# Keys scaled by POOL, a slab's low part made in pieces, a slab asked for sooner, and products of ones at the start

## The chip, the cores and the metric

The kernel runs on one core of a Trainium2 chip. The metric is the device time of one execution in microseconds. PE is TensorE, DVE VectorE, ACT ScalarE, POOL GpSimd; SP issues the transfers.

## The reference

The input is 512 rows of 1024 features in float32. The first block norms them, makes two attentions (one of a window of 128, one of a two-dimensional neighbourhood), gates and merges them, and adds a feed-forward part of width 4096. The second block runs two layers of this form:

```python
for l in range(2):
    p = rms_norm(x, norm_g[l]) @ w_in[l]
    c_q, c_kv, k_pe, z_a, u_f, z_f, g_a, g_f = split(p)
    q = rms_norm(c_q) @ w_uq                     # 8 heads x 96
    k_nope, v = split(rms_norm(c_kv) @ w_ukv)    # 8 heads x (64 + 64)
    k = concat(k_nope, k_pe for every head)      # 8 heads x 96
    q, k = rope(rms_norm(q, q_head_g)), rope(rms_norm(k, k_head_g))
    o_a = softmax(q k^T * 96**-0.5) @ v
    y_a = (o_a * silu(z_a)) @ w_attn_proj
    y_f = (real(fft2(u_f)) * silu(z_f)) @ w_fourier_proj
    m = sigmoid(g_a + b[0]) * y_a + sigmoid(g_f + b[1]) * y_f
    x = x + m @ w_out
```

## The kernel before, in words

**Split products.** Every float32 operand is split into a high part (ACT copies it to fp32r) and a low part (the difference), and each product is three passes of PE, `PASSES`. Activations lie with features on the partitions. Weights come as slabs of 128x2048 numbers, 1 MB each, numbered by `j`. Slab `j` lands in `K.raw[:, j % 2]`; ACT writes its high part to `K.w[:, j % 2, 0]` (`split`, L872) and counts `w_hi`; DVE writes the low part to `K.w[:, j % 2, 1]` (`split`, L1164) and counts `w_lo`. PE waits for `w_lo` in `slab_ready` and makes two tiles of 128x512 from most slabs (L1694), 24 products of 512 columns a tile. SP asks for slab `j` when the low part of slab `j - 2` is done, since it overwrites that buffer.

**Order.** There is no scheduler: each engine runs one list of instructions in the order of its program, and waits on counting semaphores. What stands behind a waiting instruction on its engine waits too.

**The start.** SP loads the input and the first weights in four pairs, in pieces of 0.5 MB. PE turns the input with the identity (`x_turned`, L1848), ACT and DVE split it and the weights piece by piece, and PE multiplies (`qa_part`, L1857). `K.ones` is set by POOL (L699) and first used for the sums of squares (`stat_sum`, `stat_spread`). SP's list then has slabs 2 and 3, some 25 small loads (gains, masks, rope, head gains), the bias table of the second attention through device memory in three transfers that wait for each other (zero it, write `rpb`, spread the rows), slab 4, the bias rows of two heads, and slabs 5 to 8. Tiles 4 and 5 come from slab 2, tiles 6 and 7 from slab 3, 8 and 9 from slab 4, and so on.

**A layer of block 2, to its attention.** PE makes the latents, queries (8 tiles), keys with values (8 tiles), then eight tiles from slabs `j + 5` to `j + 8`: 0 to 3 are the Fourier input, 4 to 7 the gate `z`. Meanwhile ACT squares the heads (`hsq`), DVE sums the squares (L1582), makes the roots (`head_roots`, L1565) and writes the tiles (`normed`, L1203); POOL multiplies gains in and rotates (`gain`, `rotate`), then makes `silu` of the four `z` tiles (`silu_f`, L801). The query's root is multiplied into the scores, but the keys themselves are scaled: `key_scale` on DVE (L1573), two instructions of 128x1536 numbers, after `z` tiles 5 and 6. The semaphore `head_scaled` counts the roots and both scalings. Four banks of PSUM take PE's tiles in turn, so a group can start only when DVE has emptied the one four before it.

**The Fourier stage** follows the list `FOURIER`: `dim` multiplies a group by the 128-point matrix (two banks each), `seq` by the 512-point one (slab `j + 9`, `dft_seq`), and `turn` transposes head 0's queries and keys. ACT and DVE split what `dim` gives into `ab` (L1123, L1622). At the first `seq` ACT and DVE split slab `j + 10`, which PE needs only after the attention.

**The attention** (`Heads`, kind L) has 32 steps `n`, four a head. For each, PE makes scores of 128x512, DVE scales them and finds the extreme of each row (L1302), ACT exponentiates, DVE inverts the sum (`rden`), POOL multiplies it in (`probabilities`, L718), PE transposes (`transposes`, L1778), ACT and DVE split the result (L964, L1328), and PE multiplies by the values (L1797). Heads are turned two ahead: in the step after `n % 4 == 2`, PE turns head `n // 4 + 2`. In layer 0 POOL also multiplies a tile of `x` after every even step (`scaled_x`, L742 up to step 14, L747 after it).

These are the functions that the change touches.

Of the kernel before, what the change touches and what calls it, by code (L numbers as in the profile page):

```python
# [13 lines left out]
F32 = mybir.dt.float32  # L14
# [52 lines left out]
QA_PIECES = 2 * HALF  # L67
QA_MORE = QA_PIECES - 2
J_L, JL = 57, 28
J_END = J_L + LAYERS * JL  # L70
# [22 lines left out]

KEY_SCALE = {5: 0, 6: 1}
PAR_DMAS = 6 + LAYERS * 9
# [70 lines left out]
def allocate(nc, ctx, K):  # L166
# [3 lines left out]
    def semaphore(name):  # L170
        return ctx.enter_context(nc.semaphore(name))
# [168 lines left out]
    K.head_rec = semaphore("head_rec")  # L340
    K.head_scaled = semaphore("head_scaled")
    K.rope_ok = semaphore("rope_ok")
    K.qk_ready = semaphore("qk_ready")
# [90 lines left out]
class Heads:  # L434


    def __init__(self, K, kind, layer=0):
        self.kind, self.layer = kind, layer
        self.u0 = {"AB": Num(U_A), "L": Num(U_L, (layer, UL))}[kind]
        self.s0 = {"AB": Num(S_A), "L": Num(S_L + 4, (layer, SL))}[kind]  # L440
        self.g0 = {"AB": Num(G_A), "L": Num(G_L + 40, (layer, GL))}[kind]
        self.total = len(kind) * HEADS * TT
        self.scaled = Num(3, (layer, 3))
        self.qk0 = Num(0, (layer, 2 * HEADS))
        self.f0 = Num(F_L + 40, (layer, FL)) if kind == "L" else None
        self.K = K
# [72 lines left out]
def program_sync(nc, sp, K):  # L519
# [61 lines left out]

    in_slab(2)
    in_slab(3)
    for i, gain in ((1, a["norm_mlp"][0]), (2, a["norm_final"])):
# [10 lines left out]
    for l in range(LAYERS):  # L595
# [7 lines left out]
        for q, g in enumerate((a["q_head_g_2"], a["k_head_g_2"])):  # L603
            sp.dma_start(K.head_gain[0:NOPE, q, l:l + 1], g[l][0:NOPE].rearrange("(k p) -> p k", p=NOPE),
                         allow_slow_non_contiguous=True).then_inc(K.par_in, 16)

    sp.wait_ge(K.zero_ok, 1)
    sp.dma_start(K.tab.rearrange("(p n) -> p n", p=P), K.zero[:, :]).then_inc(K.tab_zeroed, 16)
# [13 lines left out]

    in_slab(4)
    sp.wait_ge(K.rows_in, 16)
    for h in range(2):
        bias_rows(h)
    for j in range(5, 9):
        in_slab(j)
# [68 lines left out]
def program_pool(nc, pool, K):  # L697
# [13 lines left out]
    def probabilities(A):  # L711

        for n in range(A.total):
            _, _, _, lo, hi = A.where(n)
            c = slice(A.first(n), A.first(n) + (hi - lo) * P)
            pool.wait_ge(K.rden_ok, (A.u0 + n + 1).value())
            p = K.t[:, n % 3, c]
            nc.gpsimd.tensor_tensor(p, p, K.rden[:, n % 4:n % 4 + 1].broadcast_to([P, (hi - lo) * P]),  # L718
                                    ALU.mult).then_inc(K.probs_ok, 1)
            if A.kind == "L" and A.layer == 0 and n % 2 == 0:  # L720
                scaled_x(n // 2)
            if A.at(n) == "B":
                b = n - HEADS * TT
                if b == 1:
                    clear_b(0)
                if b == 3:
                    clear_b(1)
                if b // TT + 1 >= 2 and b // TT + 1 < HEADS and b % TT < 3:
                    masked(b // TT + 1, b % TT)
# [47 lines left out]
    def rotate(l, q, i):  # L777
# [18 lines left out]
        nc.gpsimd.tensor_tensor(x2, x2, ra, ALU.add).then_inc(K.rope_ok, 1)  # L796

    def silu_f(l, t):

        pool.wait_ge(K.sig_ok, (sig_num(l, t) + 1).value())  # L800
        nc.gpsimd.tensor_tensor(K.z[:, t, :], K.z[:, t, :], sig_f(K, t), ALU.mult).then_inc(K.pool_ok, 1)  # L801
# [24 lines left out]
    for l in range(LAYERS):  # L826
# [8 lines left out]
        for t in range(4):  # L835
            silu_f(l, t)
        probabilities(Heads(K, "L", l))

# [22 lines left out]
def program_act(nc, act, K):  # L861
# [201 lines left out]
    for l in range(LAYERS):  # L1063
# [26 lines left out]
        for i in range(4):  # L1090
            if i != 2:
                split(j + 6 + i, f + 20 + 2 * i)
            for k in range(2 * i, 2 * i + 2):
                for n in HEAD_SQUARES[k]:
                    q, t = divmod(n, TT)
# [63 lines left out]
def program_vector(nc, dve, K):  # L1159
# [316 lines left out]
    for l in range(LAYERS):  # L1476
# [90 lines left out]

        def key_scale(i):

            dve.wait_ge(K.rope_ok, Num(12 + 6 * (i + 1), (l, 24)).value())  # L1570
            v = K.qk[:, 1, 2 * i:2 * i + 2, :].rearrange("p t (h c) -> p (t h) c", h=HEADS)
            r = K.hr[:, 1, 2 * i * HEADS:(2 * i + 2) * HEADS]
            nc.vector.tensor_tensor(v, v, r.unsqueeze(2).broadcast_to([P, 2 * HEADS, QK]),  # L1573
                                    ALU.mult).then_inc(K.head_scaled, 1)

        for i in range(4):
            if i != 2:
                split(j + 6 + i)
            for k in range(2 * i, 2 * i + 2):
# [25 lines left out]
                if k == HEAD_ROOT:  # L1605
                    head_roots()
                if k in KEY_SCALE:
                    key_scale(KEY_SCALE[k])
        def branch_lo(grp):
# [3 lines left out]
        for stage, grp in FOURIER:  # L1613
            if (stage, grp) == ("seq", 0):
                split(j + 10)
            if stage == "dim":
# [23 lines left out]
        def za_lo(t):  # L1640
            lo(K.v[:, 1, t, :], K.t[:, t % 3, :], K.v[:, 0, t, :], h + 20 + t)

        for i in range(2):
            split(j + 11 + i)
# [27 lines left out]
def program_pe(nc, pe, K):  # L1672
# [63 lines left out]
    def turn(A, h):  # L1736

        for q in range(2):
            b = bank(A.g_qk(h) + q)
# [111 lines left out]
    def qa_part(k, t):  # L1851
# [7 lines left out]
        return mm  # L1859

    pe.wait_ge(K.ident_in, 16)
    pe.wait_ge(K.gain_in, 16)
# [3 lines left out]
    for k in range(HALF):  # L1866
# [4 lines left out]
        for i in ((2, 3), (4,), (5, 6), (7,))[k]:  # L1871
            x_turned(i)
    pe.wait_ge(K.ones_ok, 1)
    for t in range(HALF):
# [48 lines left out]
    for l in range(LAYERS):  # L1923
# [48 lines left out]
        for stage, grp in FOURIER:  # L1972
# [8 lines left out]
            elif stage == "turn":  # L1981
                pe.wait_ge(K.head_scaled, Num(3, (l, 3)).value())
                turn(heads, grp)
# [96 lines left out]
```

## Time and profile before

| | |
|---|---|
| median of three runs | 1535.9 us (1533.59 to 1538.47) |
| the profiled execution, its own time | 1537.36 us |
| its span, first to last instruction | 1535.6 us |
| mean granted clock of PE | 0.992 |
| PE busy | 1503.5 us, 98% |
| DVE busy | 818.8 us, 53% |
| ACT busy | 609.5 us, 40% |
| POOL busy | 339.1 us, 22% |
| DMA moved | 125.97 MB |

Busy is the union of an engine's instruction times. The ends of PE's instructions are modelled, so a row's length is a little more than the time to the next row's start. The granted clock is a share of full speed. "Idle before" is the time that an engine stood still ahead of an instruction, with what released it.

### The profile page before, as it was taken

To read this page: it belongs to the slowest core of one execution; us is meant where nothing else is said; L and a number is where in the kernel's file an instruction comes from. 1 tells how busy PE (TensorE), PEld (TensorE's weight loads), DVE (VectorE), ACT (ScalarE), POOL (GpSimd) and SP (SyncE) were. 2 spreads that over 40 slices of the span, in tenths; PEclk is the share of its full clock that TensorE was granted. 3 is DMA by queue.
4 is the path that set the end of the run, shared out by engine and by line. 5 is a ranking of instruction groups with operands and counts; after the bars stand their busy time and mean duration, and the time that the engine had idled before them with its cause. 6 is when DMAs were issued, how large, how long until landed. Compare 5 with 4: busy or idle time off the path is not lost.

```text
span 1535.6 us, 18967 instructions
## 1 busy us (share of the span) xinstructions
PE 1503.5 (98%) x7247; PEld 1248.4 (81%) x7247; DVE 818.8 (53%) x1324; ACT 609.5 (40%) x931; POOL 339.1 (22%) x338
## 2 busy tenths in 40 slices
PE   8899999999999999999999899999999999999998
PEld 6787788888888888888888788888888879888886
DVE  5437764344543433334578695444447879643444
ACT  5225772324331313234434575332333447533232
POOL 2004560001100000001308275110120724421012
PEclk9999999999999999999999999999999999999999
DMA  5511003332233232323232002323223200232321
GB/s 170 130 57 58 22 22 101 108 104 99 83 110 110 83 110 82 109 82 103 69 110 82 1 1 83 110 83 106 87 84 115 83 0 1 83 110 83 101 92 56
DMA packets 136478, 125.97 MB, mean 82 GB/s; under 512 B 20807, under 2 KB 132687, under 8 KB 136399
## 3 DMA queue, kind: packets, MB, share of 16 engines
q1 hardware_dynamic: 136239, 124.83, 26.1%
q8 instruction: 52, 0.85, 0.2%
q14 instruction: 27, 0.22, 0.0%
q10 hardware_dynamic: 160, 0.07, 0.0%
HBM read 122.75 MB, written 2.39 MB: 81 GB/s over the span
## 4 chain that ended last, share of the span: by engine, by line
PE 87%; DVE 6%; ACT 1%; issue 1%; SPq 1%; DMA 1%; POOL 1%; ACTq 0%; DVEq 0%; POOLq 0%
PE G L1694 67%; PE S L1676 5%; PE G L1676 5%; PE G L1797 5%; PE T L1778 3%; DVE w L1164 1%; ACT w L872 1%; PE G L1741 1%; POOL t L718 1%; PE G L1857 1%; DVE hs L1582 0%; DVE sq L1556 0%; DVE u L1177 0%; DVE sq L1302 0%; DMA raw<-in_w_in 0%
## 5 line engine op out<-in xcount | busy, mean ns | idle before, releaser
L1694 PE MATMUL G<-gx,w 128*128 128x512 f32 x3024 | 696.5, 391 | 5.2 <-DVE w L1164 5.2
L1694 PEld LDWEIGHTS G<-gx,w 128*128 128x128 f32 x3024 | 568.7, 188 | 125.4 <-DVE w L1164 5.7
L1164 DVE TENSOR_TENSOR w<-raw,w 128x2048 fp32r<-128x2048 f32 x112 | 257.6, 2300 | 236.5 <-ACT w L872 236.5
L872 ACT ACTIVATE w<-raw 128x2048 fp32r<-128x2048 f32 x112 | 211.6, 1889 | 147.8 <-PE G L1694 109.4
L1694 PE MATMUL G<-kvb,w 128*128 128x512 f32 x960 | 218.4, 389 | 0.0
L1694 PEld LDWEIGHTS G<-kvb,w 128*128 128x128 f32 x960 | 180.2, 188 | 37.4
L718 POOL TENSOR_TENSOR t<-t,rden 128x512 f32<-128x512 f32 (+2 forms) x128 | 109.5, 857 | 129.0 <-DVE rden L1308 128.7
L764 POOL TENSOR_TENSOR t<-sig 128x512 f32<-128x512 f32 x24 | 35.3, 1472 | 357.4 <-DVE sig L1377 357.4
L1429 DVE TENSOR_TENSOR x<-G,x 128x512 f32<-128x512 f32 x56 | 38.6, 689 | 114.9 <-PE G L1694 114.9
L934 ACT ACTIVATE t<-sq,nm 128x512 f32<-128x512 f32 (+3 forms) x128 | 80.2, 627 | 28.6 <-DVE nm L1302 27.7
L1694 PE MATMUL G<-m,w 128*128 128x512 f32 x384 | 87.4, 389 | 0.0
L1694 PEld LDWEIGHTS G<-m,w 128*128 128x128 f32 x384 | 72.1, 188 | 15.0
L1203 DVE SCALAR_TENSOR_TENSOR sig<-G,rstd 128x512 f32<-128x512 f32 x48 | 33.0, 687 | 95.1 <-PE G L1694 95.1
L825 POOL TENSOR_TENSOR sumsq_f<-sumsq_f,sq_f 128x512 f32<-128x512 f32 x7 | 9.1, 1299 | 333.4 <-ACT sq_f L902 333.4
L1778 PE MATMUL T<-ident,t 128*128 128x128 f32 x400 | 68.8, 284 | 4.1 <-POOL t L718 4.0
L1778 PEld LDWEIGHTS T<-ident,t 128*128 128x128 f32 x400 | 45.5, 140 | 26.0 <-POOL t L718 9.2
L972 ACT ACTIVATE sig<-sig,lp 128x512 f32<-128x512 f32 x32 | 23.2, 725 | 108.2 <-DVE sig L1203 108.2
L709 POOL TENSOR_TENSOR sumsq<-sumsq,sq 128x512 f32<-128x512 f32 x28 | 37.7, 1345 | 122.3 <-ACT sq L890 104.2
L1049 ACT ACTIVATE sq<-t 128x512 f32<-128x512 f32 x32 | 20.2, 632 | 110.8 <-DVE t L1452 110.8
L1676 PE MATMUL S<-ab 96*128 96x512 f32 x192 | 57.4, 409 | 0.7 <-DVE nm L1302 0.7
L1328 DVE TENSOR_TENSOR pt<-T,pt 128x256 fp32r<-128x256 f32 (+2 forms) x96 | 50.6, 527 | 7.1 <-ACT pt L964 3.4
L1377 DVE TENSOR_TENSOR sig<-G,sig 128x512 f32<-128x512 f32 x48 | 32.0, 687 | 40.9 <-PE G L1694 40.9
(219 smaller groups left out, 1777.4 us busy)
## 6 DMA issues: line engine op xcount, KB each, us to landing
raw<-in_w_in SPq DMA_DIRECT2D x98, 512.0 KB, 7.1
raw<-in_w_up SPq DMA_DIRECT2D x32, 512.0 KB
raw<-in_w_down SPq DMA_DIRECT2D x32, 512.0 KB
raw<-in_w_out SPq DMA_DIRECT2D x24, 512.0 KB
raw<-in_w_attn_proj SPq DMA_DIRECT2D x8, 512.0 KB
raw<-in_w_fourier_proj SPq DMA_DIRECT2D x8, 512.0 KB
xin<-in_x SPq DMA_DIRECT2D x4, 512.0 KB, 6.4
raw<-in_w_proj_a SPq DMA_DIRECT2D x8, 256.0 KB
```

What stands on the lines that cost most here:

```text
L709: nc.gpsimd.tensor_tensor(K.sumsq[:, :], K.sumsq[:, :], K.sq[:, k % 2, :], ALU.add).then_inc(K.sum_ok, 1)
L718: nc.gpsimd.tensor_tensor(p, p, K.rden[:, n % 4:n % 4 + 1].broadcast_to([P, (hi - lo) * P]), ALU.mult).then_inc(K.probs_ok, 1)
L764: nc.gpsimd.tensor_tensor(K.t[:, m, :], sig[:, m, :], sig[:, 2 + m, :], ALU.add).then_inc(K.mix_ok, 1)
L872: nc.scalar.activation(K.w[:, j % 2, 0, 0:n], K.raw[:, j % 2, 0:n], ACT.Copy).then_inc(K.w_hi, 1)
L934: nc.scalar.activation(K.t[:, n % 3, 0:width], K.sq[:, n % 2, 0:width], ACT.Exp, bias=K.nm[:, n % 4:n % 4 + 1], scale=-1.0, accum_out=K.de ...
L1164: nc.vector.tensor_tensor(K.w[:, s, 1, 0:n], K.raw[:, s, 0:n], K.w[:, s, 0, 0:n].bitcast(F32), ALU.subtract).then_inc(K.w_lo, 1)
L1328: nc.vector.tensor_tensor(K.pt[A.at(n)][m % 2][:, 1, b0:b1, e, :], K.T[(U + n) % 2][:, 0:(b1 - b0) * P].rearrange("p (k c) -> p k c", c=P) ...
L1429: nc.vector.tensor_tensor(K.x[:, k, :], psum(g)[:, :], K.x[:, k, :], ALU.add).then_inc(K.tile_out, 1)
L1676: mm = nc.tensor.matmul(bank, lhs, rhs, start=(i == 0), stop=(i == len(pairs) - 1))
L1694: mm = nc.tensor.matmul(b[:, :], w(p, k), x(q, k), start=(k == i == 0), stop=(k == kts - 1 and i == len(PASSES) - 1))
L1778: mm = nc.tensor.transpose(K.T[(U + n) % 2][:, k * P:(k + 1) * P], K.t[:, n % 3, c:c + P], K.ident[:, :])
L1797: mm = nc.tensor.matmul(out[:, :, :], v, K.pt[kind][m % 2][:, q, k, :, :], start=(i == p == q == 0), stop=(k == b1 - 1 and (p, q) == PASSE ...
```

## The change

It has four parts.

1. PE waits for the ones and multiplies them 11 times by themselves into a bank that is not read, ahead of its first transpose.
2. SP asks for slab 4 directly behind slab 3, and for slab 5 behind the small loads, ahead of the bias table; slabs 6 to 8 stay behind the first bias rows.
3. The keys of block 2 are scaled by POOL, head by head (all four row tiles of one head, 4x96 numbers a partition): heads 0 and 1 between the `silu` tiles, heads 2 to 7 within the attention. PE waits for a head's count `key_ok` when it turns it. ACT splits the slab `j + 9` ahead of its work for `z` tile 5 instead of ahead of tile 6.
4. The low part of slab `j + 10` is made by POOL in four pieces of 128x512 behind the probabilities of steps 3, 5, 7 and 9. DVE waits for it after the attention.

```diff
@@ SP
-    in_slab(2)
-    in_slab(3)
+    for j in range(2, 5):
+        in_slab(j)
...
+    in_slab(5)
     sp.wait_ge(K.zero_ok, 1)
     sp.dma_start(K.tab.rearrange("(p n) -> p n", p=P), K.zero[:, :]).then_inc(K.tab_zeroed, 16)
...
-    in_slab(4)
     sp.wait_ge(K.rows_in, 16)
     for h in range(2):
         bias_rows(h)
-    for j in range(5, 9):
+    for j in range(6, 9):
         in_slab(j)
@@ POOL, probabilities
+            if A.kind == "L" and n % TT == 1 and n // TT + 2 < HEADS:
+                key_scaled(A.layer, n // TT + 2)
+            if A.kind == "L" and n in LOW_AT:
+                slab_low(A.layer, LOW_AT.index(n))
@@ POOL
+    def key_scaled(l, h):
+
+        if h == 0:
+            pool.wait_ge(K.head_scaled, l + 1)
+            pool.wait_ge(K.rope_ok, 24 * (l + 1))
+        v = K.qk[:, 1, :, h * QK:(h + 1) * QK]
+        r = K.hr[:, 1, :].rearrange("p (t h) -> p t h", t=TT)[:, :, h:h + 1]
+        nc.gpsimd.tensor_tensor(v, v, r.broadcast_to([P, TT, QK]), ALU.mult).then_inc(K.key_ok, 1)
+
+    def slab_low(l, i):
+
+        j = Num(J_L + 10, (l, JL))
+        s, n = j % 2, SLAB // len(LOW_AT)
+        c = slice(i * n, (i + 1) * n)
+        if i == 0:
+            pool.wait_ge(K.w_hi, (j + 1 + QA_MORE).value())
+        if i == len(LOW_AT) - 1:
+            pool.wait_ge(K.w_lo, (j + QA_MORE).value())
+            pool.wait_ge(K.low_ok, (len(LOW_AT) - 1) * (l + 1))
+        nc.gpsimd.tensor_tensor(K.w[:, s, 1, c], K.raw[:, s, c], K.w[:, s, 0, c].bitcast(F32),
+                                ALU.subtract).then_inc(K.w_lo if i == len(LOW_AT) - 1 else K.low_ok, 1)
...
         for t in range(4):
             silu_f(l, t)
+            if t % 2:
+                key_scaled(l, t // 2)
@@ ACT, layers
         for i in range(4):
-            if i != 2:
+            if i < 2:
                 split(j + 6 + i, f + 20 + 2 * i)
             for k in range(2 * i, 2 * i + 2):
+                if k == 5:
+                    split(j + 9, f + 26)
@@ DVE, layers
-        def key_scale(i):
...
-                if k in KEY_SCALE:
-                    key_scale(KEY_SCALE[k])
...
-            if (stage, grp) == ("seq", 0):
-                split(j + 10)
...
+        dve.wait_ge(K.w_lo, (j + 11 + QA_MORE).value())
         for i in range(2):
             split(j + 11 + i)
@@ PE
     def turn(A, h):
 
+        pe.wait_ge(K.key_ok, HEADS * A.layer + h + 1)
...
+    pe.wait_ge(K.ones_ok, 1)
+    for _ in range(WARM):
+        nc.tensor.matmul(K.G[0][:, 0:P], K.ones[:, :], K.ones[:, :], start=True, stop=True)
     pe.wait_ge(K.ident_in, 16)
...
-                pe.wait_ge(K.head_scaled, Num(3, (l, 3)).value())
                 turn(heads, grp)
```

`WARM` is 11 and `LOW_AT` is (3, 5, 7, 9). DVE's first wait in the attention is for one count of `head_scaled` a layer, where it was three.

## Rows read from the trace of the kernel before

**Rows 1.** PE's waits over the whole kernel: total, times, longest.
```profile
PE G L1694 <- DVE w L1164: 5.2, 1, 5.2
...
PE G L1676 <- DVE z L1203: 4.5, 4, 1.2
PE T L1778 <- POOL t L718: 4.0, 9, 1.1
```

**Rows 2.** timeline: start, us, engine, line, names, shapes, count [idle before <-releaser].
```profile
0.83 0.20 POOL L699 MEMSET ones<- 128x128 f32 x1
...
5.03 0.24 PE L1863 MATMUL G<-ident,t 8*128 8x8 f32 x1 [5.03 <-DMA t<-in_norm_mix]
...
8.64 5.21 PE L1857 MATMUL G<-gx,w 128*128 128x512 f32 x12 [1.47 <-DVE w L1171]
...
14.48 3.00 PE L1857 MATMUL G<-gx,w 128*128 128x512 f32 x12
...
34.27 1.10 PE L1734 MATMUL S<-sq,ones 128*128 128x512 f32 x2
```

**Rows 3.** timeline from 30 to 66 us, around slab 4.
```profile
30.05 2.29 DVE L1164 TENSOR_TENSOR w<-raw,w 128x2048 fp32r<-128x2048 f32 x1 [2.50 <-ACT w L872]
...
37.97 11.04 PE L1694 MATMUL G<-gx,w 128*128 128x512 f32 x48
...
47.59 0.58 SPq L608 DMA_DIRECT2D bias_table<-zero  x1
...
53.91 1.60 SPq L530 DMA_DIRECT2D raw<-in_w_in  x2
...
61.31 1.91 ACT L872 ACTIVATE w<-raw 128x2048 fp32r<-128x2048 f32 x1 [10.70 <-DMA raw<-in_w_in]
```

**Rows 4.** PE in four stretches: busy us (count), granted clock, DMA share, GB/s.
```profile
8.60:13.80 5.20, 5.16 (x14) 1.00 0.99 368
65.60:71.50 5.90, 5.90 (x14) 0.50 0.57 178
...
853.30:859.80 6.50, 5.25 (x13) 0.50 0.00 0
```

**Rows 5.** timeline of layer 0, into the Fourier stage.
```profile
844.38 1.75 DVE L1573 TENSOR_TENSOR qk<-qk,hr 128x1536 f32<-128x1536 f32 x1
...
850.18 0.95 PE L1676 MATMUL G<-sw,u 128*128 128x256 f32 x6 [1.03 <-DVE z L1203]
...
852.36 1.08 PE L1676 MATMUL G<-sw,u 128*128 128x256 f32 x6 [1.23 <-DVE z L1203]
852.99 1.64 ACT L1123 ACTIVATE ab<-G 128x256 fp32r<-128x256 f32 x4
...
854.69 5.42 PE L1676 MATMUL G<-w,ab 128*128 128x512 f32 x12 [1.25 <-DVE ab L1622]
```

**Rows 6.** timeline of PE in the same stage of layer 1.
```profile
1238.70 1.58 PE L1676 MATMUL G<-sw,u 128*128 128x256 f32 x6 [1.23 <-DVE z L1203]
1240.89 5.19 PE L1676 MATMUL G<-w,ab 128*128 128x512 f32 x12 [0.62 <-DVE ab L1622]
```

**Rows 7.** POOL by form: names, shapes, count | busy us, mean ns | idle.
```profile
L718 POOL TENSOR_TENSOR t<-t,rden 128x512 f32<-128x512 f32 x64 | 66.4, 1039 | 85.8 <-DVE rden L1308 85.7
...
L718 POOL TENSOR_TENSOR t<-t,rden 128x384 f32<-128x384 f32 x16 | 13.7, 857 | 9.9 <-DVE rden L1308 9.9
L793 POOL TENSOR_TENSOR qk<-qk,rope 128x256 f32<-128x256 f32 x8 | 11.3, 1410 | 0.0
...
L747 POOL TENSOR_TENSOR x<-x,sumsq 128x512 f32<-128x512 f32 x8 | 10.3, 1294 | 0.0
```

**Rows 8.** timeline of layer 0's attention, POOL's probabilities and PE's transposes.
```profile
879.18 2.04 POOL L718 TENSOR_TENSOR t<-t,rden 128x512 f32<-128x512 f32 x2 [0.16 <-DVE rden L1308]
...
881.47 0.60 PE L1778 MATMUL T<-ident,t 128*128 128x128 f32 x4
...
898.05 0.60 PE L1778 MATMUL T<-ident,t 128*128 128x128 f32 x4
```

More of the change, by code:

```diff
@@ L68 @@
 QA_MORE = QA_PIECES - 2
+WARM = 11
 J_L, JL = 57, 28
@@ L92 @@
 HEAD_ROOT = 4
-KEY_SCALE = {5: 0, 6: 1}
+LOW_AT = (3, 5, 7, 9)
 PAR_DMAS = 6 + LAYERS * 9
@@ L341, in allocate @@
     K.head_scaled = semaphore("head_scaled")
+    K.key_ok = semaphore("key_ok")
+    K.low_ok = semaphore("low_ok")
     K.rope_ok = semaphore("rope_ok")
@@ L442, in __init__ @@
         self.total = len(kind) * HEADS * TT
-        self.scaled = Num(3, (layer, 3))
+        self.scaled = Num(1, (layer, 1))
         self.qk0 = Num(0, (layer, 2 * HEADS))
@@ L1566, in head_roots @@
             nc.vector.tensor_scalar(K.hr[:, 0, :], K.hr[:, 0, :], -float(QK) ** -0.5, None, ALU.mult).then_inc(K.head_scaled, 1)
-        def key_scale(i):
[L1570 to L1574, printed above, removed]
         for i in range(4):
@@ L1872, in program_pe @@
             x_turned(i)
-    pe.wait_ge(K.ones_ok, 1)
     for t in range(HALF):
```

## The prediction

> **What bounds the kernel now.** I read the page's busy shares first: TensorE (PE) is busy 98% of the span, so a change can only pay where PE stands idle or runs at its lower clock. The table of PE's waits names the places [rows 1]: one wait of 5.2 us for a weight slab, 5.0 us at the start for the first data, 4.5 us in four waits of the Fourier stage for tiles `z`, and 4.0 us in nine waits for POOL's probabilities. The chain of waits agrees: outside these places it is PE nearly throughout. The granted clock adds what the waits hide [rows 4]: after the slab's wait PE works at 0.50 (1.2 GHz) from 65.6 to 71.5 us, and in the Fourier stage of layer 0 from 853.3 to 859.8. Idle time there is paid twice.
>
> **Part 1, products of ones.** The ones are there at 1.03 us, the first transpose starts at 5.03 and the first real products at 8.64 [rows 2]. Twelve of these take 5.21 us (434 ns each), the next twelve 3.00 (250 ns): the first twelve run at half speed, though the granted clock's column reads 1.00 there [rows 4]. If the ones bring the clock up in time, 5.21 - 3.00 = 2.2 us go. What they cost: no 128x128 product of plain float32 stands in the trace. The nearest is the 128x512 one of the statistics, 1.10 us (two records) at the full clock [rows 2]; a quarter of its columns is 0.28 us, some 0.5 at half clock, so eleven take between 3 and 5 us. From about 1.1 us on they end between 4.1 and 6.2, against 5.03 for the transpose behind them: a delay of 0 to 1.2 us. Between the first transposes and 8.64 PE idles for ACT and DVE, as before, and there the clock may fall again. The part is thus worth -2.2 to +1.2 us. I take -0.6, nearer to nothing, because the clock also fell in the Fourier stage after gaps of only 1.03, 1.23 and 1.25 us [rows 5].
>
> The Trainium skill (TensorE: Matmul & The Clock Gate, Part 1, What's actually happening) says that the low clock is the default and that activity lifts it. The twelve slow products agree. By that rule alone the part would give its whole 2.2 us; this is a rival below.
>
> **Part 2, slabs 4 and 5.** Slab 4 reuses the buffer that DVE's low part of slab 2 frees at 30.05 + 2.29 = 32.3 us. Yet SP asks for it at 53.91, behind some 25 small loads and the bias table's three dependent ones [rows 3]. It lands at 61.3; ACT (1.91) and DVE (2.29) split it, and PE starts at 65.60 after 5.23 us idle [rows 3]. In the new order it is asked for at 32.4, and takes 7 to 8 us. ACT reaches its split once the tiles of slab 2 are converted, at about 50.6, and DVE is done at 54.8. PE wants it at 60.4: 5.6 us to spare. So the 5.2 us go, and with them the low clock of 5.9 us behind, worth half of that, 2.9. Sum: -8.1 us.
>
> What becomes late instead: SP now waits at slab 4 until 32.3, and two issues take 1.1 us, so the small loads end 5.6 us later, at 53.1. Slab 5 is asked for there and lands at about 61; it is wanted 11 us after 60.4 (48 products take 11.04 [rows 3]), and is split by 67. The bias table's chain (47.59 to 56.9 before) starts at 54.2 behind slab 5's 1 MB, and ends near 66. Slab 6 follows at 67.6, lands at 75 and is split by 79.3; PE wants it at 82.4. It is the tightest: 3 us. POOL's first bias sums, which read those rows, start only at 120 us. The clear of `pt` that waits for the zeroed table was at 50.7 and its successor waits until 120, so ten microseconds later is free.
>
> **Part 3, keys off DVE, ACT's split sooner.** In layer 0 DVE stands between PE and the Fourier stage: a key scaling of 1.75 us at 844.38, then the wait for ACT's half of the `dft_seq` slab (845.04 to 846.94), DVE's low part, tile `z` 6, the second scaling, tile 7 [rows 5]. PE's banks come free with these tiles: it idles 1.03 and 1.23 us, then 1.25 for `ab`, and its twelve products of the first `seq` take 5.42 us [rows 5], where twelve of the same width take 3.00 at the full clock [rows 2]. Lost: 3.51 + 2.42 = 5.9 us. In layer 1 the waits on `z` are what is left of the four, 4.5 - 1.03 - 1.23 = 2.24 us [rows 1], the one on `ab` is 0.62, the products take 5.19, and six of 256 columns take 1.58 [rows 6] instead of 0.95 [rows 5]: 2.86 + 2.19 + 0.63 = 5.7 us.
>
> After: ACT splits at 842.2 to 844.1, as soon as its fourth sigmoid is out. DVE makes tile 5 until 844.5, the slab's low part until 846.9, tile 6 until 847.6, and tile 7, whose products end at 847.7, until 848.6. ACT's last sigmoid is over at 849.3, and the products of `seq` begin 1.7 us behind that, as they did before (852.99 to 854.69 [rows 5]), at 851.0. PE's own work (two groups of 1.43 us behind 847.6) ends at 850.5. So 0.5 us of idle is left and the clock should stay. Gains: 5.4 us in layer 0, 5.2 in layer 1. POOL's scalings of heads 0 and 1 between the `silu` tiles end near 852, turn 0 comes at about 864, and DVE needs the `silu` tiles only after the first `seq`: hidden.
>
> **Part 4, POOL inside the attention.** POOL gets in each layer six key scalings (heads 2 to 7, behind probabilities 1, 5, ... 21) and four pieces of 128x512 of the slab's low part (behind 3, 5, 7, 9). The slab's low part leaves DVE (2.29 us at the first `seq`), where it was not on PE's path: nothing gained. For a piece the nearest row is L747, two full operands of 128x512 in the same attention: 1.29 us. For a scaling of 384 numbers a row it is L718 with 128x384: 0.86 [rows 7]; back to back POOL loses 0.04 less each, so 1.25 and 0.82.
>
> PE takes 8.3 us for a head; POOL before needs 4 x 1.0 for probabilities and in layer 0 2 x 1.0 for `x`. With a scaling and two pieces it has 9.3. The slack is small where these come: probabilities 1 and 2 end at 881.2, PE transposes the second of them at 881.47 [rows 8], and every fourth one from 5 on is as close. In layer 0 POOL would work without a pause from 879.2 until probability 10 is done: ten probabilities (10.0), four `x` (4.0), three scalings (2.5), four pieces (5.0), in all 21.5, to 900.7. PE's transposes 10 stood at 898.05 [rows 8], so PE comes 2.8 us later. Behind that the load is 8.3 a head at most, with slack again. In layer 1, without the `x`, I go through it: scaling 2 ahead of probability 2 costs 0.6, scaling plus piece ahead of probability 6 another 0.3, ahead of 10 another 0.3: 1.2 us. With a scaling at 1.04 (a row of 128x512) and a piece at 1.41 (L793, slowed by DVE [rows 7]) the two layers cost 4.0 and 2.1; with both as cheap as a probability, piece 1.0 and scaling 0.75, they cost 1.6 and 0.7. The middle stands because L747 is the same operation in the same place.
>
> A page speaks to the piece's price. The Trainium skill (GPSIMD Engine Reference, Performance versus the Vector engine) has 4497 ns for an add of 2048 elements; an estimate of a quarter is 1.12 us against the row's 1.29. By it the sum would be 0.7 us lower in layer 0; the row decides.
>
> **The sum.** -0.6 - 8.1 - 5.4 - 5.2 + 2.8 + 1.2 = -15.3 us. The profiled execution took 1537.4 us (span 1535.6), so 1522.1 for it; it lies 1.5 over the median of 1535.9. For the median I say 1520.6.
>
> **Rivals.**
> (a) The clock falls anyway in the layers: the 0.5 us of idle, or the stalls at the attention's thin start, where PE works in short groups. A fall costs what it cost in the Fourier stage, 2.2 to 2.4 us for the products behind it; two of them give 1525.
> (b) Slab 6 or 5 becomes the late one. For: SP's order puts the table's chain ahead of slab 6 and only 3 us are to spare. Against: the chain was 9.3 us with a slab among it. With a wait of 3 us and the clock down behind it (2.9) the time is 1526.5.
> (c) The ones give all: 1519.
> (d) The other side: POOL is stretched by DVE. L793 averages 1.41 us for 128x256 numbers [rows 7], since some of them run beside DVE's big subtractions. DVE is busy nine tenths of the attention. If each of the seven added POOL instructions of a layer's first ten steps took 1.3 us more, PE would come 9 us later a layer, 18 in all: 1538, slower. It decides from 1.1 us more on each. Against: all 64 probabilities of the two layers average 1.04 beside that same DVE [rows 7].
> (e) The DVE chain is only reshuffled, the Fourier stage still waits for ACT's sigmoids and keeps half its loss: 1526.
>
> **How the numbers follow.** My forecast with its own range of 1517 to 1524 has 0.56; (a) 0.14, (b) 0.09, (c) 0.09, (d) 0.03, (e) 0.09. Lowest: all of the ones (-1.6 more) and cheap POOL (-1.7 more) give 1517.3; highest without (d): dear POOL (+2.1) with (a) or (b) gives 1527 to 1529. I state 1515.5 to 1528. A measurement of this kernel tells 0.3%, 4.6 us, from no change. Every case but (d) ends below 1531.3, so faster has 0.94; two mishaps together could end within the bound, 0.04; slower 0.02.
>
> **What would show it.** Right: no wait of PE for a slab, granted clock 1.00 from 60 to 76 us; no waits on `z` of a microsecond in the Fourier stages and the first `seq` in 2.9 us; waits on POOL grown to some 5 us in layer 0's attention, placed at transposes 2, 5, 6, 9 and 10. The first twelve products read the clock of part 1 by their duration. Wrong: a new wait for L1164 near 71 or 82 us, POOL pieces over 1.5 us, or the low clock again behind `dim`.

## The result, and the profile after

The changed kernel takes 1521.5 us in the median of four runs (1519.02 to 1523.6), the kernel before 1537.1 (1533.59 to 1538.47). The ratio is 0.9906, with an interval of 0.9886 to 0.9925: about 15 us faster, where 15.3 were forecast. The profiled execution is the slowest of the four: 1523.6 us, span 1521.8, against 1537.36 and 1535.6 before.

The table cuts the two profiled executions at the same pieces of PE's work, and sets the forecast's terms beside the differences.

| stretch, by the first instruction of PE | before, us | after, us | difference | forecast |
|---|---|---|---|---|
| start, to slab 2's products | 37.97 | 37.51 | -0.46 | -0.6 |
| slab 2 to the first attention's scores | 82.83 | 74.53 | -8.30 | -8.1 |
| first attention, to the merge | 106.25 | 110.37 | +4.12 | none |
| layer 0, eight tiles to the second `seq` | 57.80 | 51.51 | -6.29 | -5.4 |
| layer 0, from there to the attention's end | 82.03 | 84.48 | +2.45 | +2.8 |
| layer 1, eight tiles to the second `seq` | 57.38 | 51.36 | -6.02 | -5.2 |
| layer 1, from there to the attention's end | 80.45 | 81.21 | +0.76 | +1.2 |
| all else | 1030.89 | 1030.83 | -0.06 | 0 |

The sum is -13.8 us, the difference of the spans. The first attention was not in the sum. The terms that were forecast give -17.9 together, 2.6 us more than the -15.3.

PE's waits of the changed kernel (total, times, longest) answer to [rows 1]:

```profile
PE T L1801 <- POOL t L721: 6.1, 15, 1.1
PE G L1880 <- DVE w L1204: 2.1, 2, 1.9
...
PE G L1886 <- POOL ones L702: 1.1, 1, 1.1
...
PE G L1698 <- DVE ab L1643: 0.3, 1, 0.3
```

The slab's wait of 5.2 us and the four waits for `z` are gone from the list. Waits for POOL have grown from 4.0 us in nine to 6.1 in fifteen.

The timeline of the same kernel, start and slabs, answers to [rows 2] and [rows 3]:

```profile
1.09 4.75 PE L1886 MATMUL G<-ones 128*128 128x128 f32 x22 [1.09 <-POOL ones L702]
5.77 0.22 PE L1889 MATMUL G<-ident,t 8*128 8x8 f32 x1
...
8.89 4.53 PE L1880 MATMUL G<-gx,w 128*128 128x512 f32 x12 [1.88 <-DVE w L1204]
...
52.37 1.16 SPq L533 DMA_DIRECT2D raw<-in_w_in  x2
53.57 0.49 SPq L612 DMA_DIRECT2D bias_table<-zero  x1
...
51.98 2.29 DVE L1197 TENSOR_TENSOR w<-raw,w 128x2048 fp32r<-128x2048 f32 x1 [1.63 <-ACT w L903]
63.21 2.29 DVE L1197 TENSOR_TENSOR w<-raw,w 128x2048 fp32r<-128x2048 f32 x1 [1.91 <-ACT w L903]
74.51 2.29 DVE L1197 TENSOR_TENSOR w<-raw,w 128x2048 fp32r<-128x2048 f32 x1 [1.91 <-ACT w L903]
```

The eleven products of ones (two records each) end at 5.8 and delay the first transpose by 0.74 us. The first twelve real products still take 4.53 us, where they took 5.21 [rows 2]. The three DVE rows are slabs 4, 5 and 6: split at 54.3, 65.5 and 76.8, while PE reaches them near 60, 71 and 82. All three come some 5 us ahead, slab 6 too, for which the prediction gave 3.

The windows of PE, PEld (PE's loads of weights), DVE, ACT and POOL (busy, count), then the granted clock, the DMA share and GB/s, answer to [rows 4]:

```profile
60.00:76.00 16.00, 16.00 (x72) 13.28 (x71) 7.60 (x8) 5.51 (x5) 0.00 (x0) 1.00 0.56 165
...
121.50:135.00 13.50, 13.34 (x47) 10.36 (x48) 6.87 (x30) 6.22 (x19) 4.56 (x7) 0.50 0.11 30
...
848.00:860.00 12.00, 12.00 (x70) 10.47 (x69) 5.32 (x9) 4.91 (x10) 0.00 (x0) 1.00 0.01 1
```

The clock is up around slab 4 and in the Fourier stage, where it was 0.50 before. But at the beginning of the first attention it lies at 0.50 for 13.7 us, with PE busy for nearly all of it. The kernel before has 3.4 us of low clock there, from 132.9 to 136.3:

```profile
133.00:136.00 3.00, 3.00 (x13) 2.56 (x13) 2.10 (x8) 2.04 (x6) 1.51 (x3) 0.50 0.00 0
```

The timeline of the layers answers to [rows 5], [rows 6] and [rows 8]:

```profile
842.89 3.03 PE L1698 MATMUL G<-sw,u 128*128 128x256 f32 x24
...
846.17 2.99 PE L1698 MATMUL G<-w,ab 128*128 128x512 f32 x12 [0.25 <-DVE ab L1643]
...
850.88 2.91 PE L1698 MATMUL G<-w,ab 128*128 128x512 f32 x12
...
871.11 0.66 PE L1801 MATMUL T<-ident,t 128*128 128x128 f32 x4 [0.45 <-POOL t L721]
...
877.36 0.66 PE L1801 MATMUL T<-ident,t 128*128 128x128 f32 x4 [0.33 <-POOL t L721]
880.41 0.66 PE L1801 MATMUL T<-ident,t 128*128 128x128 f32 x4 [0.28 <-POOL t L721]
...
886.65 0.66 PE L1801 MATMUL T<-ident,t 128*128 128x128 f32 x4 [0.32 <-POOL t L721]
889.71 0.66 PE L1801 MATMUL T<-ident,t 128*128 128x128 f32 x4 [0.27 <-POOL t L721]
...
1228.58 2.97 PE L1698 MATMUL G<-w,ab 128*128 128x512 f32 x12
```

The twenty-four products of `dim` run in one piece, and the first `seq` takes 2.99 us for 5.42. In the attention PE waits at transposes 2, 5, 6, 9 and 10, where it did not before. Its waits for POOL there come to 3.9 us in nine, where the prediction looked for some 5; before they were 2.3 us in four.

POOL by form (count, busy us, mean ns, idle before) answers to [rows 7]:

```profile
L721 POOL TENSOR_TENSOR t<-t,rden 128x512 f32<-128x512 f32 x64 | 66.3, 1040 | 62.7 <-DVE rden L1341 62.5
...
L812 POOL TENSOR_TENSOR qk<-qk,hr 128x384 f32<-128x384 f32 x16 | 13.4, 836 | 0.0
...
L824 POOL TENSOR_TENSOR w<-raw,w 128x512 fp32r<-128x512 f32 x8 | 10.3, 1290 | 0.0
```

A scaling costs 0.84 us, a piece 1.29, as priced.

### The profile page after: what moved, and what is told of

Read it like the earlier page. It is cut to its first block, busy times and chain, and to the rows that moved or that the text cites. A ratio compares the mean times of both kernels' runs of the same rounds, so it can differ in the third digit from the quotient of the medians.

```text
span 1521.8 us, 19049 instructions
## 1 busy us (share of the span) xinstructions
PE 1502.4 (99%) x7269; PEld 1248.4 (82%) x7269; DVE 808.5 (53%) x1318; ACT 609.9 (40%) x931; POOL 360.7 (24%) x362
## 4 chain that ended last, share of the span: by engine, by line
PE 92%; POOL 3%; DVE 3%; ACT 1%; issue 1%; DVEq 0%; ACTq 0%; POOLq 0%
PE G L1716 73%; PE G L1698 5%; PE S L1698 5%; PE G L1820 4%; PE T L1801 3%; POOL t L721 2%; PE G L1880 1%; POOL w L824 1%; PE G L1764 1%; DVE sq L1335 0%; POOL qk L812 0%; PE G L1886 0%; DVE xout L1691 0%; DVE gx L1214 0%; POOL x L749 0%
## 5 line engine op out<-in xcount | busy, mean ns | idle before, releaser
L1197 DVE TENSOR_TENSOR w<-raw,w 128x2048 fp32r<-128x2048 f32 (+1 forms) x110 | 252.7, 2297 | 222.4 <-ACT w L903 222.4
```

The lines of the kernel that those rows point to most:

```text
L1197: nc.vector.tensor_tensor(K.w[:, s, 1, 0:n], K.raw[:, s, 0:n], K.w[:, s, 0, 0:n].bitcast(F32), ALU.subtract).then_inc(K.w_lo, 1)
```

## The experiments

**The parts alone.** Each of these is the kernel before with one part of the change.

`a1_slabs`: the order of the slabs only.

```diff
-    in_slab(2)
-    in_slab(3)
+    for j in range(2, 5):
+        in_slab(j)
...
+    in_slab(5)
     sp.wait_ge(K.zero_ok, 1)
...
-    in_slab(4)
     sp.wait_ge(K.rows_in, 16)
...
-    for j in range(5, 9):
+    for j in range(6, 9):
         in_slab(j)
```

> The kernel before with the new order of slabs 4 and 5 alone. My theory (the wait for slab 4 and the low clock behind it): PE's products of slab 4 start 8 to 8.3 us sooner and nothing is late behind them, 1527 to 1530 us. The rival that slab 6 becomes late: a wait of about 3 us at slab 6, near 82 us, and 1532 or more. What the first attention's start gives back by a longer low clock is to be seen here too: up to 4 us.

Measured: 1530.57 us in ten runs (1525.82 to 1533.21), ratio 0.9977 (0.9962 to 0.9992). In its trace, slab 2 to the attention takes 74.53 us, 8.3 less than before, as in the changed kernel, with no wait for a slab. Yet the median gives some 3.5 us of that. Windows of this kernel in the first attention:

```profile
121.50:128.00 6.50, 5.87 (x21) 4.19 (x22) 4.69 (x21) 4.00 (x13) 2.89 (x5) 0.59 0.10 30
128.00:135.00 7.00, 7.00 (x42) 5.54 (x42) 4.31 (x17) 4.30 (x13) 2.52 (x4) 0.89 0.10 28
```

The low clock is 6.8 us long here. The trace itself was one of the better executions (span 1525.5, mean clock 0.997); the clock of the ten runs goes from 0.990 to 0.997. The layers of this kernel are those of before, yet its trace has no low clock in layer 0's Fourier stage, which takes 55.33 us for 57.80, and 3.4 us of it in layer 1, 56.87 for 57.38.

The traces with the old order of slabs go far to show why the median gives less. The wait for slab 4 and the length of the low clock behind it differ among them, though no edit touches that stretch:

| trace | wait for slab 4, us | low clock behind it, us | slab 2 to the first attention, us |
|---|---|---|---|
| before | 5.2 | 6.8 | 82.83 |
| `a2_keys` | 4.9 | 6.8 | 82.50 |
| `a3_low` | 4.5 | 3.4 | 80.86 |
| `a4_ones` | 3.8 | 3.4 | 80.07 |
| `a5_fill` | 3.0 | 0 | 77.86 |

Against 74.53 us the new order is worth 3.3 to 8.3 us. The wait is gained in every execution; what the clock adds differs from one to the next.

`a2_keys`: the keys on POOL and ACT's earlier split, no pieces; slabs and ones as before.

```diff
         for t in range(4):
             silu_f(l, t)
+            if t % 2:
+                key_scaled(l, t // 2)
...
+            if A.kind == "L" and n % TT == 1 and n // TT + 2 < HEADS:
+                key_scaled(A.layer, n // TT + 2)
...
-            if i != 2:
+            if i < 2:
                 split(j + 6 + i, f + 20 + 2 * i)
             for k in range(2 * i, 2 * i + 2):
+                if k == 5:
+                    split(j + 9, f + 26)
...
-                if k in KEY_SCALE:
-                    key_scale(KEY_SCALE[k])
```

> The kernel before with the keys scaled by POOL and ACT's earlier split, the low part left on DVE. Theory: 6.0 us gained in each Fourier stage, 0.5 to 1 us lost in each attention for the scaling ahead of probability 2; 1524 to 1527 us. Rival (the Fourier stage is held by the sigmoids as well): 3 us a layer, 1530.

Measured: 1525.2 us (1522.14 to 1526.57), ratio 0.9937 (0.9913 to 0.9962). The Fourier stretches are 51.53 and 51.39, the whole gain of both layers (-6.3 and -6.0). The attentions are 82.65 and 81.04: +0.62 and +0.59.

`a3_low`: the pieces alone.

```diff
+            if A.kind == "L" and n in LOW_AT:
+                slab_low(A.layer, LOW_AT.index(n))
-            if (stage, grp) == ("seq", 0):
-                split(j + 10)
```

> The kernel before with only the low part moved to POOL in four pieces inside the attention. Theory: nothing is gained in the Fourier stage, since DVE's low part there is not on PE's path; layer 0 loses 1 to 2 us and layer 1 less than 0.5: 1537 to 1539 us. Rival: DVE's 2.3 us at the first seq were on the path and it gains 1 us or more a layer.

Measured: 1537.47 us (1530.98 to 1539.27, ten runs), ratio 1.0005 (0.9988 to 1.0023). The Fourier stretches stay (58.13 and 57.34); the attentions take 82.60 and 80.43, that is +0.57 and nothing. Keys alone and pieces alone add 1.2 us in layer 0; together they cost 2.45. Each part alone costs 0.6 us or less a layer; in layer 0 both together cost twice the sum of the two.

`a4_ones`: eleven products of ones alone.

```diff
+    pe.wait_ge(K.ones_ok, 1)
+    for _ in range(11):
+        nc.tensor.matmul(K.G[0][:, 0:P], K.ones[:, :], K.ones[:, :], start=True, stop=True)
     pe.wait_ge(K.ident_in, 16)
```

> The kernel before with only the eleven products of ones. Theory: the clock is up before the gap ahead of the first real products and falls within them, so the tile of slab 2 starts 0 to 1 us sooner than before; no difference that the times can tell, 1534 to 1538. Rival (the ones keep the clock up): the first twelve products take 3.0 us and it gains 2 us.

Measured: 1535.63 us (1531.62 to 1537.37, ten runs), ratio 1.0004 (0.9988 to 1.002): nothing. Over the traces, the second twelve products start at 14.48, 14.48, 14.44 and 14.93 without ones, and at 14.05, 14.10, 14.51, 14.68 and 14.87 with the eleven ones. A sixth trace with them, that of `b4_late_act` below, has 12.36: there the ones gave all that the prediction's rival (c) asks for.

**Which half of part 3 does it.** `b4_late_act`: the changed kernel with ACT's split of slab `j + 9` at its old place (a single run).

```diff
-            if i < 2:
+            if i != 2:
                 split(j + 6 + i, f + 20 + 2 * i)
             for k in range(2 * i, 2 * i + 2):
-                if k == 5:
-                    split(j + 9, f + 26)
```

> The changed kernel with ACT's split of the slab j + 9 back where it was, ahead of tile z 6 (POOL still scales the keys). Theory: DVE waits for ACT's 1.9 us behind the sigmoid of tile 5, so tile 6 comes some 2 us later and PE idles about 1 us more a layer, perhaps with the clock down behind it: 1 to 3 us a layer from its first z tile to the second seq. Rival: moving the scalings alone carries the gain, 0.3 us or less.

Measured: 1523.7 us. Its PE waits:

```profile
PE G L1696 <- DVE ab L1641: 2.2, 2, 1.2
PE G L1696 <- DVE z L1234: 2.2, 2, 1.1
```

The stretches are 53.77 and 53.61 us. So the earlier split is worth 2.25 us a layer. What comes back is idle time, 4.4 us of waits over the two layers; the clock stayed up in this execution. The other 4.0 and 3.8 us came with the scalings' leave from DVE, but not all of that is DVE's time: `a1_slabs` had layer 0 at 55.33 us with nothing changed there and the clock up, only 1.6 over this kernel. Some 2.5 us of layer 0's gain is thus the low clock, which some executions of the old order do not have.

The start of this trace is the one that stands apart:

```profile
1.09 4.57 PE L1884 MATMUL G<-ones 128*128 128x128 f32 x22 [1.09 <-POOL ones L702]
8.72 3.00 PE L1878 MATMUL G<-gx,w 128*128 128x512 f32 x12 [1.88 <-DVE w L1202]
```

The same eleven ones and the same 1.88 us of idle time stand ahead of the first products as in the changed kernel, but these take 3.00 us where they took 4.53.

**Slab 5's place.** `c1_slab4_only`: the changed kernel with slab 5 asked for behind the bias table's chain (a single run).

```diff
-    in_slab(5)
     sp.wait_ge(K.zero_ok, 1)
...
-    for j in range(6, 9):
+    for j in range(5, 9):
         in_slab(j)
```

> The changed kernel with slab 5 back behind the bias table's chain, slab 4 still asked for directly behind slab 3. Theory: slab 5 lands near 68 us, is split by 72.5 and PE wants it at 71: a wait of 0 to 2 us. Rival (a slab in the table's chain slows it, so taking it out makes all earlier): no wait, and the chain of the table ends sooner.

Measured: 1524.87 us, with a new wait of PE. Its timeline:

```profile
53.12 0.58 SPq L611 DMA_DIRECT2D bias_table<-zero  x1
...
61.05 1.28 SPq L624 DMA_DIRECT2D rawb<-bias_rows  x2
62.38 11.24 SPq L533 DMA_DIRECT2D raw<-in_w_in  x6
70.35 2.29 DVE L1196 TENSOR_TENSOR w<-raw,w 128x2048 fp32r<-128x2048 f32 x1 [8.57 <-ACT w L902]
...
72.70 3.48 PE L1715 MATMUL G<-gx,w 128*128 128x512 f32 x14 [1.43 <-DVE w L1196]
```

PE waits 1.43 us for slab 5, and the stretch takes 76.29 us for 74.53. So slab 4 alone would have passed the lateness on to slab 5. Without a slab in its midst the table's chain takes 7.9 us from the zeroing to the first row's load; in the changed kernel it takes 10.6 (53.57 to 64.14), which harms nothing.

**POOL's work ahead of the attention.** `r_after` is the changed kernel again, run beside the next three. 

> The changed kernel once more, beside the three below on one chip. Theory: the first attention's length differs between executions with where the low clock falls (106 to 110.4 us from its start to the merge), the rest of the trace repeats within 0.3 us; 1519 to 1524 us. Rival: the long stretch of low clock in the first attention belongs to the change and comes again, 13 us long.

 Measured: 1520.31 us (1518.68 to 1524.15), ratio 0.9908 (0.9883 to 0.9934), attentions 84.43 and 81.16. Windows of its first attention:

```profile
121.50:128.00 6.50, 5.78 (x21) 3.87 (x21) 4.94 (x20) 3.73 (x12) 3.14 (x4) 0.63 0.11 30
128.00:135.00 7.00, 7.00 (x41) 5.56 (x39) 3.99 (x17) 4.17 (x12) 2.26 (x3) 0.85 0.12 30
```

The same program has 6.8 us of low clock here and 13.7 in the first profile; the first attention takes 107.58 us for 110.37.

`b1_early`: the six scalings and four pieces of a layer straight behind the `silu` tiles.

```diff
         for t in range(4):
             silu_f(l, t)
             if t % 2:
                 key_scaled(l, t // 2)
+        for h in range(2, HEADS):
+            key_scaled(l, h)
+        for i in range(len(LOW_AT)):
+            slab_low(l, i)
```

and both calls are taken out of `probabilities`.

> The changed kernel with all that POOL was given put ahead of the attention, where it idles 18.8 us: scalings of heads 2 to 7 (5 us) and the four pieces (5.2 us) behind the silu tiles. Theory: each attention gets back what it lost, 2.4 us in layer 0 and 0.8 in layer 1, and the Fourier stage stays as it is; some 3 us under the changed kernel, 1517 to 1520. Rival: the pieces, which read two full operands, now meet DVE's subtractions in the Fourier stage and slow both, so that the gain is given back there.

Measured: 1515.97 us (1515.61 to 1518.6), ratio 0.9877 (0.9859 to 0.9895). Timeline of POOL and DVE in layer 0:

```profile
845.18 4.81 POOL L808 TENSOR_TENSOR qk<-qk,hr 128x384 f32<-128x384 f32 x6
849.95 5.93 POOL L820 TENSOR_TENSOR w<-raw,w 128x512 fp32r<-128x512 f32 x4
864.06 1.04 POOL L721 TENSOR_TENSOR t<-t,rden 128x512 f32<-128x512 f32 x1 [8.17 <-DVE rden L1341]
...
849.13 1.41 DVE L1210 TENSOR_TENSOR u<-t,u 128x512 fp32r<-128x512 f32 x1 [0.70 <-ACT u L947]
```

POOL is done at 855.9 and then idle for 8.2 us, so the room was there. The attentions fall to 82.02 and 80.46, the times of before: POOL's 2.4 and 0.7 us are gone. The median is 4.3 us under the changed kernel beside it and below the range that was expected; these 3.1 us explain most of that, and the rest stays open. A piece is 1.42 us here and one DVE instruction is stretched to 1.41 (0.69 in the changed kernel), but the Fourier stretches stay at 51.54 and 51.55.

**Where the clock falls.** `b2_gap`: `b1_early`, and eight more ones between the first transposes and the first products.

```diff
+    for _ in range(8):
+        nc.tensor.matmul(K.G[0][:, 0:P], K.ones[:, :], K.ones[:, :], start=True, stop=True)
     for k in range(HALF):
         for t in range(HALF):
             mm = qa_part(k, t)
```

> b1_early with eight more products of ones between the first transposes and the first real products, where PE idles 1.9 us. Theory: the clock stays up, the first twelve products take 3.0 us instead of 4.5, and the products of slab 2 start 1.3 us sooner. Rival: the eight themselves delay the first real product by what they take too long, and nothing is won.

Measured: 1516.14 us (1515.44 to 1518.74), ratio 0.9878 (0.986 to 0.9896). Timeline of PE:

```profile
7.54 1.95 PE L1893 MATMUL G<-ones 128*128 128x128 f32 x16
9.59 2.97 PE L1880 MATMUL G<-gx,w 128*128 128x512 f32 x12
...
13.19 3.01 PE L1880 MATMUL G<-gx,w 128*128 128x512 f32 x12
```

Now the first twelve take 2.97 us, so the clock is up, and the second twelve start at 13.19, 1.5 us sooner than in `b1_early` (14.68). `b3_thin` and `a5_fill` below, which have the eight as well, repeat it: 2.98 and 3.01 us, with the second twelve at 12.44 and 12.18. But the total is unchanged: this trace has 10.2 us of low clock in the first attention, which takes 109.11 us for 107.62.

`b3_thin`: `b2_gap`, and three ones ahead of the first transposes and three ahead of the next scores of the first attention.

```diff
+        def filled():
+
+            if A.kind == "AB":
+                pe.wait_ge(K.tile_out, (A.g_out(0) - GB + 1).value())
+                for _ in range(3):
+                    nc.tensor.matmul(K.G[A.g_out(0) % GB][:, 0:P], K.ones[:, :], K.ones[:, :], start=True, stop=True)
...
+            if n == 1:
+                filled()
             if n + AHEAD < total:
                 scores(n + AHEAD)
+            if n == 0:
+                filled()
             transposes(n)
```

> b2_gap with three products of ones ahead of the transposes of step 0 and three ahead of the scores in step 1 of the first attention, where PE waits 0.6 and 0.7 us. Theory: the clock no longer falls at the start of the first attention, which takes 105 us instead of 106 to 110 in every execution: 1 to 4 us. Rival: what brings the clock down there is all of the thin start, latencies of DVE, ACT and POOL, and 1.3 us of ones do not keep it up: no gain, and up to 1.3 us lost.

Measured: 1513.28 us (1512.64 to 1513.66), ratio 0.986 (0.9842 to 0.9878): the fastest version, 7.0 us under the changed kernel beside it. Windows of its first attention, and then the two places of the ones in the timeline:

```profile
110.00:135.00 25.00, 24.51 (x142) 19.31 (x142) 18.04 (x69) 14.11 (x39) 14.51 (x19) 1.00 0.08 24
135.00:150.00 15.00, 15.00 (x97) 11.78 (x95) 12.14 (x44) 11.02 (x32) 6.35 (x9) 1.00 0.11 28
```

```profile
118.26 0.94 PE L1829 MATMUL G<-ones 128*128 128x128 f32 x6
119.03 0.38 PE L1801 MATMUL T<-ident,t 128*128 128x128 f32 x2
119.25 0.83 PE L1829 MATMUL G<-ones 128*128 128x128 f32 x6
```

The clock stays at 1.00 where it was 0.50, the attention takes 104.69 us, and the four runs lie within 1.0 us of each other.

`a5_fill`: the kernel before with all these ones (eleven, eight, three and three) and nothing else.

```diff
+    for _ in range(11):
+        nc.tensor.matmul(K.G[0][:, 0:P], K.ones[:, :], K.ones[:, :], start=True, stop=True)
     pe.wait_ge(K.ident_in, 16)
...
+    for _ in range(8):
+        nc.tensor.matmul(K.G[0][:, 0:P], K.ones[:, :], K.ones[:, :], start=True, stop=True)
     for k in range(HALF):
...
+            if n == 1:
+                filled()
             if n + AHEAD < total:
                 scores(n + AHEAD)
+            if n == 0:
+                filled()
             transposes(n)
```

> The kernel before with ones alone: the eleven at the start, eight in the gap behind the first transposes, three and three in the first attention's thin start; slabs, keys and low part as before. Theory: the low clock at the start and in the first attention is an item of its own, beside those behind slab 4 and in the Fourier stages, which stay; the attention takes 105 us, 1.5 to 2 us come at the start, and the whole gains 3 to 5 us over before. Rival: the ones help only where the other stalls are gone: no difference.

Measured: 1530.07 us (1526.94 to 1531.63, ten runs), ratio 0.9967 (0.9953 to 0.9981). Its wait for slab 4, and its windows:

```profile
PE G L1694 <- DVE w L1164: 3.0, 1, 3.0
...
64.00:71.00 7.00, 7.00 (x33) 5.79 (x32) 3.49 (x3) 1.92 (x2) 0.00 (x0) 1.00 0.57 180
115.00:135.00 20.00, 19.96 (x116) 15.60 (x115) 13.90 (x56) 11.16 (x33) 11.16 (x15) 1.00 0.07 20
845.00:860.00 15.00, 14.17 (x63) 11.97 (x64) 8.55 (x12) 6.72 (x11) 0.45 (x1) 0.80 0.00 1
```

The first attention takes 104.72 us with the clock up, so the ones do this by themselves. Their work does not reach the layers: the Fourier stretches stay at 57.78 and 57.39, with the clock down again. The slab's wait was 3.0 us here and no low clock followed it. In the ten runs against the kernel before the ones give some 5 us, and none of what the change does in the layers. The trace alone can't share these out, since the stretch of slab 4, which holds none of the ones, was 5.0 us shorter than in the trace of before.

## Why the prediction was right, step by step

**Slabs: right.** The wait of 5.2 us and the low clock behind it went: -8.3 for -8.1. Slab 4 was split at 54.3 (forecast 54.8), slab 6 at 76.8 (79.3). Rival (b) did not come; `c1_slab4_only` shows that it would have come with slab 5 left behind the chain. What the sum had wrong is the standing of its second half: in `a1_slabs` the trace has the 8.3 us and the median some 3.5. The prediction priced the wait and the clock from one trace, and among five traces with the old order that one is at the top (the gain would be 3.3 to 8.3). That the term came out within 0.2 us owes much to one execution of the kernel before being both what the prediction read and what the result is compared with here.

**Fourier stages: right in mechanism, 0.8 us too small each.** No wait for `z`, 0.25 us at `ab`, `seq` in 2.99. The second `seq` starts at 850.88, as forecast (851.0). The cut of the table reaches to that second `seq` and so holds all that the prediction counted; forecast were -5.4 and -5.2, measured -6.3 and -6.0. In layer 0 the `seq` gave the 2.4 us that it was priced at. The rest lies ahead of it: from the first product of `dim` to the first `seq` PE took 7.13 us before, 3.51 of them idle, and 3.28 after, 0.25 of them idle. So 0.25 comes from the idle time that is left (0.5 in the forecast), and 0.59 from the products themselves, 3.62 us in three broken groups and 3.03 in one piece: each pause cost 0.2 us beyond the idle time that stands in its row. A small part of that is the clock, which was down from 853.1, within the last group; in `a1_slabs`, with the clock up, the same three groups took 3.52 us, 0.16 a pause. Rival (e) is out. `b4_late_act` shows that both edits are needed: 2.25 us for the split, and 4.0 for the scalings in an execution with the clock down before, 1.6 in one with the clock up. The 2.4 us of the `seq` is a price that not every execution pays: `a1_slabs` has this `seq` in 3.01 us with the stage unchanged.

**POOL in the attention: right.** +2.45 for +2.8, +0.76 for +1.2. The places are the five that were worked out, and the prices of 0.84 and 1.29 are those of the nearest rows. The 1.12 us that the prediction estimated for a piece from the Trainium skill (GPSIMD Engine Reference, Performance versus the Vector engine) was too low. PE's waits for POOL in layer 0 grew by 1.6 us and not by the 2.8 that the sign asks for; the other 0.8 of the 2.45 us does not stand in the waits. Rival (d) is out: beside DVE's work no piece was stretched. `a2_keys` and `a3_low` show that half of the cost comes from the two together, and `b1_early` that it need not be paid.

**Ones: right that they give little.** -0.46 for -0.6 in the profile, and nothing that ten runs can tell. Eleven products at the prediction's 0.5 us would be 5.5 us and not 5; they took 4.39 to 5.07 in the nine traces that have them. The reason, that the clock may fall in the idle time behind the ones, holds for most executions and not for all: with 1.88 us idle, five traces have the first twelve products in 4.53 to 4.58 us, and `b4_late_act` has them in 3.00. So rival (c), the whole 2.2 us, came true in one trace of six. With eight more ones in the gap the first twelve took 3.0 us in three of three (`b2_gap`, `b3_thin`, `a5_fill`), and the second twelve start 1.3 to 2.3 us sooner than in the kernel before. The small gain in the changed kernel's profile is therefore in part chance: what the eleven ones give depends on the execution.

**What was missing: the first attention.** The prediction treated everything between 82 and 840 us as unchanged. Before, 3.4 us of low clock lay at the start of the first attention; in the profile of the changed kernel 13.7, which cost 4.1 us. It is rival (a)'s mechanism at another place. Over all thirteen traces the stretch follows the length of the low clock:

| traces | low clock, us | first attention, us |
|---|---|---|
| `b3_thin`, `a5_fill` | 0 | 104.69, 104.72 |
| before, `a2_keys` | 3.4 | 106.25, 106.19 |
| `a1_slabs`, `a3_low`, `a4_ones`, `b1_early`, `b4_late_act`, `r_after` | 6.8 | 107.52 to 107.63 |
| `b2_gap`, `c1_slab4_only` | 10.2 | 109.11, 109.23 |
| after | 13.7 | 110.37 |

That is some 0.42 us for each microsecond. Since the same program had 13.7 and 6.8 us, this is no fixed price of the change; in the median the part is smaller (the profiled run is 2.1 us over it). The forecast for the median came out near because this loss and the 2.6 us more from the other terms partly cancel; that closeness is luck, though the mechanisms of the terms are shown. Open stays why the low clock lasts longer in some executions, and whether the changed kernel meets the long ones more often than the one before. Without ones at this place, the seven traces with the new order of slabs have 6.8 to 13.7 us and the four with the old order 3.4 to 6.8; that leans towards yes, and is not shown by so few. The two kernels with ones at this place have no low clock there in their traces, and the first attention then runs 1.6 us faster than in the trace of before.

## What to carry to other kernels

Where PE is busy 98% of the time, look at every place where it works in short groups behind idle time: a few products of ones there can save some microseconds and narrow the spread (2.9 us in the median from `b2_gap` to `b3_thin`, and four runs within 1.0 us). When work is moved to an engine with slack, look for the stretch where it is idle for long (here the 8 us before the attention), and not for gaps between its urgent instructions; two additions that each fit can cost double together. Price a stall at low clock from several traces before it goes into a sum: the same stall cost 3.3 us in one execution here and 8.3 in another. When a transfer is asked for sooner, check the one behind it: moving only the late one passes the wait on.

## What the runs showed of the hardware

The granted clock at one place differs between executions of the same kernel: 13.7 and 6.8 us at 0.50 in two profiles of the changed kernel. The 25 runs of the kernel before beside `a1_slabs` spread from 1529.66 to 1538.41 us, with mean clocks from 0.990 to 0.997. The Trainium skill (TensorE: Matmul & The Clock Gate, Part 1, What's actually happening) calls the ramp run-variable; these traces agree (first twelve products in 4.53 to 4.58 us in five traces and 3.00 in one, behind the same ones and the same idle time), and show it in mid-kernel as well.

The column of the granted clock reads 1.00 at the start of the kernel before, where twelve products take 5.21 us [rows 2]; `b2_gap` has 2.97 for the same twelve. Until the record's first change, durations tell the clock better than the column.

Eleven plain float32 products of 128x128 take 4.75 us at the start of the changed kernel (0.43 each; 4.39 to 5.07 over nine traces), and eight behind them take 1.95 (0.24 each), with the clock up by the duration of the products that follow.
